# First norm by plain transposes, attention in pairs of banks, and values from high and low parts of the probabilities side by side

## The reference, cut to what matters

```
mod = silu(c) @ w_mod[l] + b_mod[l]
shift, scale, gate = split(mod, 3)
h = rms_norm(x, g_pre[l]) * (1.0 + scale) + shift
... = split(h @ w_in_e)                       # 2560 columns: GLA, latent attention, gates

s = einsum('qhd,khd->hqk', qn, kn) + einsum('qhr,kr->hqk', qr, kr)    # 4 heads, 2048 x 2048
p = softmax(s)
o = einsum('hqk,khd->qhd', p, v) * silu(z)
```

## Time and profile before

| | us |
|---|---|
| median of 3 runs | 3141.64 |
| lowest and highest run | 3140.18, 3143.88 |
| the profiled execution, its own time | 3143.72 |
| its span, first to last instruction | 3141.9 |
| PE busy | 3020.9 (96%) |
| DVE busy | 1365.7 (43%) |
| ACT busy | 1171.1 (37%) |
| POOL busy | 655.5 (21%) |

### The profile page before, as it was taken

How to read it: one execution, slowest core, us unless ns; L and a number is a source line. 1 busy time by engine, 2 the same in 40 slices (tenths; PEclk the granted TensorE clock), 3 DMA queues, 4 the chain that set the end, 5 groups by cost and what they waited for, 6 DMA issues and landing times.

```text
span 3141.9 us, 47947 instructions
## 1 busy us (share of the span) xinstructions
PE 3020.9 (96%) x17252; PEld 2534.5 (81%) x17252; DVE 1365.7 (43%) x2431; ACT 1171.1 (37%) x2092; POOL 655.5 (21%) x614
## 2 busy tenths in 40 slices
PE   4899999999899999998999999999999999999999
PEld 4668888888788888887878888888888888877887
DVE  5276777755676776673434111122222222222011
ACT  3462244555455555553235111232332332322111
POOL 2111211256222222221320001011211211113221
PEclk8999999999999999999999999999999999999999
DMA  6233345596221111122643211121121121134231
GB/s 228 71 118 97 109 153 160 161 285 197 74 58 54 53 54 53 54 58 91 207 167 118 94 74 50 61 81 60 60 80 60 60 80 60 53 134 160 95 107 53
DMA packets 259929, 317.65 MB, mean 101 GB/s; under 512 B 17187, under 2 KB 187299, under 8 KB 257220
## 3 DMA queue, kind: packets, MB, share of 16 engines
q1 hardware_dynamic: 259814, 316.10, 30.9%
HBM read 213.67 MB, written 102.37 MB: 101 GB/s over the span
## 4 chain that ended last, share of the span: by engine, by line
PE 87%; issue 4%; POOL 3%; DVE 3%; ACT 2%; DMA 1%; SPq 0%; POOLq 0%; DVEq 0%; ACTq 0%
PE PS L349 12%; PE PS L351 11%; PE PS L350 11%; PE PS L2287 4%; PE PS L2288 4%; PE PS L2289 4%; PE PS L2438 4%; PE PS L2439 4%; PE PS L2440 4%; PE PS L1739 4%; PE PS L1759 2%; PE PS L1760 2%; PE PS L1761 2%; PE PS L1728 2%; PE PS L1729 2%
## 5 line engine op out<-in xcount | busy, mean ns | idle before, releaser
L349 PE MATMUL PS<-hTh,whi 128*128 128x512 f32 x1664 | 661.1, 397 | 26.1 <-DVE hTl L302 15.7
L351 PE MATMUL PS<-hTh,wlo 128*128 128x512 f32 x1664 | 652.1, 392 | 0.0
L350 PE MATMUL PS<-hTl,whi 128*128 128x512 f32 x1664 | 652.0, 392 | 0.0
L349 PEld LDWEIGHTS PS<-hTh,whi 128*128 128x128 f32 x1664 | 315.1, 189 | 99.8 <-issue 15.2
L351 PEld LDWEIGHTS PS<-hTh,wlo 128*128 128x128 f32 x1664 | 315.0, 189 | 66.7
L350 PEld LDWEIGHTS PS<-hTl,whi 128*128 128x128 f32 x1664 | 315.5, 190 | 63.7 <-issue 0.2
L341 POOL TENSOR_TENSOR whi<-wraw,zero 128x1024 fp32r<-128x1024 f32 x52 | 100.2, 1928 | 1205.8 <-PE PS L351 953.3
L1832 ACT ACTIVATE pb__168<-PS,nm,rq 128x512 f32<-128x512 f32 x256 | 197.5, 780 | 130.1 <-DVE nm L1896 130.1
L2287 PE MATMUL PS<-ow_h,of_h 128*128 128x512 f32 x576 | 225.0, 391 | 7.5 <-DVE oy L2242 7.5
L2288 PE MATMUL PS<-ow_l,of_h 128*128 128x512 f32 x576 | 224.8, 390 | 0.0
L2289 PE MATMUL PS<-ow_h,of_l 128*128 128x512 f32 x576 | 224.7, 390 | 0.0
(11 more groups left out here) (268 smaller groups left out, 5850.5 us busy)
## 6 DMA issues: line engine op xcount, KB each, us to landing
projT<-pev SPq DMA_DIRECT2D x80, 256.0 KB, 2.7
xt<-x SPq DMA_DIRECT2D x8, 2048.0 KB, 9.4
mw<-wmod SPq DMA_DIRECT2D x64, 256.0 KB, 2.8
oxt<-x SPq DMA_DIRECT2D x32, 512.0 KB, 4.8
sg_v<-vev SPq DMA_DIRECT2D x64, 256.0 KB, 2.4
wraw<-wuz SPq DMA_DIRECT2D x32, 512.0 KB, 6.0
vm<-sg_v SPq DMA_DIRECT2D x16, 1024.0 KB, 5.6
sgT<-mT SPq DMA_DIRECT2D x16, 1024.0 KB, 4.4
```

The costliest lines, as they stand in the source:

```text
L349: pe.matmul(PS[:, bank, :], w[1][:, s, k, :], hTh[:, k, b], start=(k == 0), stop=False)
L350: pe.matmul(PS[:, bank, :], w[1][:, s, k, :], hTl[:, k, b], start=False, stop=False)
L351: mm = pe.matmul(PS[:, bank, :], w[2][:, s, k, :], hTh[:, k, b], start=False, stop=(k == KD - 1))
```

## The change

It has three parts.

**Start.** `norm_pool_scale` and `ndiag` are gone. DVE scales x in place (`norm_dve_scale`, which layer 1 already used) and PE does plain transposes. A block of the first eight waits for each feature step by itself. PE does all eight steps of a group's transposes together, after the second block of a pair. ACT squares the next group between steps 3 and 4 of a group. The first two weight tiles are loaded before the last four rows of w_mod; ACT makes their high part and DVE the low one. The rows for the gates are loaded later, and the modulation's buffers lie in a free part of hTh.

**Order of the attention.** PE: S0 S1 T0 T1 S2 S3 T2 T3 V0 V1, then S0 S1 T0 T1 S2 S3 shares V2 V3 T2 T3. ACT and DVE follow.

**Values and shares.** High and low parts lie side by side in `pt`, so a key step is a 512-wide matmul (v high by both parts) and a 256-wide one (v low by the high part). High-by-high and high-by-low land in two halves of bank 6; DVE multiplies each half by the gate and adds them (three instructions in place of one), and the next values wait for the two multiplications (`s_oa`). `diag` is split by POOL in `dgh` and `dgl`, and the shares are two 256-wide float32r matmuls.

```diff
-        macc0 = at("macc0", X0, [P, 2 * D])
-        mw0 = at("mw0", X0 + 8 * K, [P, 4, D])
+        macc0 = at("macc0", H0 + 36 * K, [P, 2, 2 * D])
+        mw0 = at("mw0", H0 + 4 * K, [P, 4, 2 * D])
...
-        def norm_pool_scale(pool, g):
-            pool.wait_ge(s_rs, 2 * g + 2)
-            if g:
-                pool.wait_ge(s_tp, 8 * g)
-            for t in range(4):
-                r = 40 + 4 * (g % 2) + t
-                pool.tensor_tensor(ndiag[:, t, :], ident[:, :], small[:, r:r + 1].broadcast_to([P, P]), ALU.mult).then_inc(s_xn, 1)
...
-                if g < 4:
-                    mm = pe.matmul(o, x, ndiag[:, t, :], start=True, stop=True)
-                else:
-                    mm = pe.transpose(o, x, ident[:, :])
+                mm = pe.transpose(o, x, ident[:, :])
...
             for k in range(KD):
+                if normed is not None:
+                    pe.wait_ge(s_hl, normed + k + 1)
...
+        def first_split_act(act, g):
+            act.wait_ge(s_wr[g], 16)
+            act.activation(whi0[:, g, :, :].rearrange("p k c -> p (k c)"), wraw0[:, g, :], ACT.Copy).then_inc(s_whi, 1)
+
+        def first_split_dve(dve, g):
+            dve.wait_ge(s_whi, g + 1)
+            dve.tensor_tensor(wlo0[:, g, :, :].rearrange("p k c -> p (k c)"), wraw0[:, g, :],
+                              whi0[:, g, :, :].rearrange("p k c -> p (k c)").bitcast(F32), ALU.subtract).then_inc(s_wlo, 1)
...
             for m in range(8):
                 norm_act(act, m)
+            norm_act_front(act, 1)
             for g in range(1, 4):
-                norm_act_front(act, g)
                 proj_evict(act, 2 * g - 2)
-                for k in range(6):
+                proj_evict(act, 2 * g - 1)
+                for k in range(8):
                     norm_act(act, 8 * g + k)
-                proj_evict(act, 2 * g - 1)
-                for k in range(6, 8):
-                    norm_act(act, 8 * g + k)
+                    if k == 3 and g < 3:
+                        norm_act_front(act, g + 1)
...
             for n in range(2 * KD):
                 mod_sum(dve, n)
+                if n == 4:
+                    norm_dve_scale(dve, 0)
+                if n == MOD_CUT:
+                    first_split_dve(dve, 0)
+                if n == MOD_CUT + 1:
+                    first_split_dve(dve, 1)
             mod_end(dve, 0)
             norm_dve(dve, 0)
             for g in range(1, 4):
+                norm_dve_scale(dve, g)
                 norm_dve(dve, g)
...
             for j in range(8):
                 proj_block(pe, j)
-                g = j // 2 + 1
-                if g < 4:
-                    for k in (range(6, 8) if j % 2 else range(6)):
-                        norm_pe(pe, 8 * g + k)
+                if j % 2 and j < 7:
+                    for k in range(8):
+                        norm_pe(pe, 4 * j + 4 + k)
...
-                for u in range(2):
-                    mm = pe.matmul(PS[:, 7, u * P:(u + 1) * P], ones[:, :], diag[:, u, :], start=True, stop=True)
-                mm.then_inc(s_rb, 1)
+                both = ones[:, :].bitcast(F32R)
+                pe.matmul(PS[:, 7, 0:2 * P], both, dgh[:, :, :].rearrange("p u c -> p (u c)"), start=True, stop=False)
+                pe.matmul(PS[:, 7, 0:2 * P], both, dgl[:, :, :].rearrange("p u c -> p (u c)"), start=False, stop=True
+                          ).then_inc(s_rb, 1)
...
-                    o, tok = PS[:, 6, 0:2 * P], slice(k * P, (k + 1) * P)
-                    pe.matmul(o, vh[:, tok], pth[:, k, :], start=(k == 0), stop=False)
-                    pe.matmul(o, vh[:, tok], ptl[:, k, :], start=False, stop=False)
-                    mm = pe.matmul(o, vl[:, tok], pth[:, k, :], start=False, stop=(k == NT - 1))
+                    tok = slice(k * P, (k + 1) * P)
+                    pe.matmul(PS[:, 6, :], vh[:, tok], pt[:, k, :, :].rearrange("p a q -> p (a q)"), start=(k == 0), stop=False)
+                    mm = pe.matmul(PS[:, 6, 0:2 * P], vl[:, tok], pt[:, k, 0, :], start=False, stop=(k == NT - 1))
...
-                dve.tensor_tensor(ost[:, :], PS[:, 6, 0:2 * P], mzt[:, :], ALU.mult).then_inc(s_oe, 1)
+                dve.tensor_tensor(ost[:, :], PS[:, 6, 0:2 * P], mzt[:, :], ALU.mult).then_inc(s_oa, 1)
+                dve.tensor_tensor(mzt[:, :], PS[:, 6, 2 * P:4 * P], mzt[:, :], ALU.mult).then_inc(s_oa, 1)
+                dve.wait_ge(s_oa, I * 2 + (E_oa + 5))
+                dve.tensor_tensor(ost[:, :], ost[:, :], mzt[:, :], ALU.add).then_inc(s_oe, 1)
...
                 pool.tensor_tensor(diag[:, u, :], ident[:, :], rinv[:, u:u + 1].broadcast_to([P, P]), ALU.mult).then_inc(s_dg, 1)
+                pool.wait_ge(s_dg, N * 3 + 7)
+                pool.tensor_tensor(dgh[:, u, :], diag[:, u, :], zero[:, 0:1].broadcast_to([P, P]), ALU.add).then_inc(s_dg, 1)
+                pool.wait_ge(s_dg, N * 3 + 8)
+                pool.tensor_tensor(dgl[:, u, :], diag[:, u, :], dgh[:, u, :].bitcast(F32), ALU.subtract).then_inc(s_dg, 1)
```

More of the change, by code:

```diff
@@ L172, in mod_sum @@
                 dve.wait_ge(s_macc, n)
-            acc = macc0[:, half * D:(half + 1) * D]
-            dve.scalar_tensor_tensor(acc, mw0[:, n % 4, :], cvec[:, k:k + 1], acc, ALU.mult, ALU.add).then_inc(s_macc, 1)
+            acc = macc0[:, half, 0:D]
+            dve.scalar_tensor_tensor(acc, mw0[:, n % 4, 0:D], cvec[:, k:k + 1], acc, ALU.mult, ALU.add).then_inc(s_macc, 1)
         def mod_cols(pe, acc, half):
-            for j in range(half * KD, half * KD + KD):
-                mm = pe.matmul(PS[:, 0, j:j + 1], acc[:, j * P:(j + 1) * P], ones[:, 0:1], start=True, stop=True)
+            for k in range(KD):
+                j = half * KD + k
+                mm = pe.matmul(PS[:, 0, j:j + 1], acc[:, k * P:(k + 1) * P], ones[:, 0:1], start=True, stop=True)
             return mm
@@ L184, in mod_pe @@
                 pe.wait_ge(s_macc, KD * (half + 1))
-                mm = mod_cols(pe, macc0, half)
+                mm = mod_cols(pe, macc0[:, half, 0:D], half)
             mm.then_inc(s_mps, 1)
@@ L391, in start_sp @@
             norm_load(sp, 0, (0,))
-            for n in range(2 * KD):
+            for n in range(MOD_CUT):
+                mod_load(sp, n)
+            for g in range(2):
+                proj_load(sp, g)
+            for n in range(MOD_CUT, 2 * KD):
                 mod_load(sp, n)
@@ L395, in start_sp @@
             sp.wait_ge(s_macc, 2 * KD)
-            for g in range(2):
-                proj_load(sp, g)
+            gate_rows(sp)
             norm_load(sp, 0, (2,))
@@ L406, in start_act @@
             norm_act_front(act, 0)
+            for g in range(2):
+                first_split_act(act, g)
             for m in range(8):
                 norm_act(act, m)
+            norm_act_front(act, 1)
             for g in range(1, 4):
-                norm_act_front(act, g)
                 proj_evict(act, 2 * g - 2)
-                for k in range(6):
+                proj_evict(act, 2 * g - 1)
+                for k in range(8):
                     norm_act(act, 8 * g + k)
-                proj_evict(act, 2 * g - 1)
-                for k in range(6, 8):
-                    norm_act(act, 8 * g + k)
+                    if k == 3 and g < 3:
+                        norm_act_front(act, g + 1)
             proj_evict(act, 6)
@@ L432, in start_pool @@
             pool.wait_ge(s_const, 48)
-            norm_pool_front(pool, 0)
-            norm_pool_scale(pool, 0)
-            pool.wait_ge(s_mps, 1)
-            for g in range(2):
-                proj_split(pool, g)
-            for g in range(1, 4):
+            for g in range(4):
                 norm_pool_front(pool, g)
-                norm_pool_scale(pool, g)
         def start_pe(pe):
@@ L1609, in emit @@
         pb_ = at("pb_", M0 + 111 * K, [P, 2, S])
-        pth = at("pth", M0 + 127 * K, [P, NT, 2 * P], F32R)
-        ptl = at("ptl", M0 + 143 * K, [P, NT, 2 * P], F32R)
+        pt = at("pt", M0 + 127 * K, [P, NT, 2, 2 * P], F32R)
+        dgh = at("dgh", M0 + 64 * K, [P, 2, P], F32R)
+        dgl = at("dgl", M0 + 65 * K, [P, 2, P], F32R)
         qraw = at("qraw", M0 + 68 * K, [P, 2, 2, P])
@@ L1666, in emit @@
         s_oe = sem("s_oe")
+        s_oa, E_oa = s_bk, NT
         s_mlg = sem("s_mlg")
@@ L1708, in mod1_pe @@
             for half in range(2):
-                mod_cols(pe, macc1, half)
+                mod_cols(pe, macc1[:, half * D:(half + 1) * D], half)
             for bank, src in ((1, macc1[:, 2 * D:2 * D + 512]), (2, macc1[:, 2 * D + 512:]), (3, maccg[:, 0:512]), (4, maccg[:, 512:])):
@@ L1783, in pieces @@
                                 piece_pe(pe, n)
-                    for b in range(2):
-                        scores(h, N, u, (b,))
-                        turn_if(b)
+                    scores(h, N, u, (0, 1))
+                    turn_if(0)
+                    turn_if(1)
                     if u:
```

65 lines of the change are left out of this document (31 added, 34 removed).

## The result

| | before | after |
|---|---|---|
| median, runs (us) | 3140.93, 4 runs | 3112.91, 4 runs |
| lowest to highest | 3140.18 to 3143.88 | 3108.08 to 3116.9 |
| the profiled execution | 3143.72 | 3112.22 |
| its span | 3141.9 | 3110.4 |

What follows compares the result with a forecast made beforehand. TensorE holds 87% of the chain, so its list sets the time nearly everywhere. Attention 13.8 us plus start 12.3 make 26.1 us saved, giving 3115.5 us by the median, range 3104 to 3131.

Steps and rivals of the forecast that it cites:

- Values, 0.13 us a pair: Attention values on PE: a 512-wide and a 256-wide matmul per key step save 16 issues, 0.13 us a pair.
- Rival 4: Attention: wide value steps held by weight loads, narrow shares costing as float32; 3127 to 3130 us, chance 0.11 with rival 2.
- Shares, 0.20: Attention shares on PE: two 256-wide float32r matmuls take 0.24 us, saving 0.20 us a pair.
- Waits for the low part, 0.10: Attention turns on PE: the paired order leaves nothing of the 0.10 us a pair spent waiting for VectorE's low part.
- Changing between turns and scores costs PE nothing: Attention on PE: 1.16 us of scores plus 0.44 of transposes make the 1.60 measured, so pairing saves no switching price.
- GpSimd, 0.3 us of room: Attention: with two more GpSimd instructions, the query split still ends 0.3 us before PE's next first scores, at no cost.
- VectorE's room: Attention: despite two more instructions, VectorE's low parts are read some 0.3 to 0.7 us before the turns need them.
- rival 2: Attention: VectorE late, third and fourth turns wait 0.4 us a pair, no attention gain; 3129 us, chance 0.11 with Rival 4.
- Until the modulation, +1.2 us: Start: VectorE's added scalings and subtractions end the modulation 1.2 us after 43.94 us, bounds 0 and 2.6.
- First group: Start: low-part contention between VectorE and POOL goes; transposes of the second group start at 63.5 us, against 66.45.
- Groups 2 to 4, 59.8 and 3 us for the clock: Start: groups take 21.5, 21.5 and 16.8 us, plus 1 us each for half clock; eighth block ends at 126.3.
- rival 1: Start: half clock through all three second blocks loses 14.7 us, so the start gives 0.6; 3127 us, chance 0.13.

Runs made afterwards that it cites:

- the added operation: The changed kernel with one more GpSimd operation of 128 columns behind each low part of the inverse sums, result unused: 3122.75 us.
- the variant of three moves: Changed kernel with low parts behind VectorE's last modulation sum, second group's squares before the first norm, six next-group transposes between a group's two blocks: 3106.88 us.
- the one of two moves: The variant of three moves with the low parts of the first weight tiles put back between VectorE's modulation sums: 3104.62 us.
- the kernel with the whole wait: The changed kernel, but the first block of a group waits for all eight norm steps, as before, not step by step: 3136.82 us.
- the store moved: The variant of three moves with the first block's result stored before the last 2 MB of x are loaded, not behind them: 3103.88 us.

## Why the prediction was right, and where its steps were off

The forecast was 3115.5 us in a range of 3104 to 3131; 3112.9 was measured, faster, by the mechanisms it named. That the two are so near is in part luck. Between the two profiled executions the gain is 31.5 us and the sum had 26.1: the pairs gave 3.0 us more than forecast, the start 0.6, and the stages outside both 1.7, for which the sum had nothing. Step by step:

- **Values, 0.13 us a pair.** 0.13 by the two periods 18.68 and 18.55. Held. Rival 4 did not come: a key step takes 0.35 us and the shares 0.24.
- **Shares, 0.20.** 0.20 by 18.88 and 18.68. Held.
- **Waits for the low part, 0.10.** 0.10, at the one turn named above. Held.
- **"Changing between turns and scores costs PE nothing"** was the sentence that failed, and it made pairing them worth nothing in the sum. I had read it from one turn and one run of five scores, and could not see there that in runs of ten the later steps are shorter. That gave another 0.10 us a pair: it came out at 18.55 and not 18.65, 3 us of the kernel.
- **What the sum hid.** The three terms were added as if each stood alone. They don't: the values and the shares are worth nothing without the order. The total was near because all three were made together; the prediction has no sentence that says so.
- **GpSimd, 0.3 us of room.** 0.11 by the added operation. The chain from the shares to the end of the split came within 0.1 us of what I had worked out (3.63 us from 1117.54 to 1121.17, where I had 3.55), and I had left out the handing over (0.12 us from the split's end to the scores where PE waits). Right in kind, close to wrong in effect: a quarter of a microsecond more on GpSimd would have cost 4 to 5 us (0.14 by 32).
- **VectorE's room.** From 860 to 1390 us no wait of PE for the low part is left; rival 2 did not come.
- **Until the modulation, +1.2 us.** It was +3.1, beyond my bound of 2.6: I had priced VectorE's two subtractions (which stand three and two sums from the end, not four), and not that w_mod's rows arrive behind the weight tiles. In the variant of three moves, with the subtractions behind the last sum, it was still 45.5: 1.6 us for the rows, and 1.5 for the subtractions.
- **First group.** ACT's start to group 2's transposes was 17.4 us (47.26 to 64.66) where I had 18.2. With the later modulation the transposes came at 64.66 instead of 63.5.
- **Groups 2 to 4, 59.8 and 3 us for the clock.** 60.9 in all: 22.8, 21.6 and 16.5. The half clock struck in the first blocks' pauses (0.77 over 75 to 90 us) and not through the second blocks, which took 5.8, 5.5 and 5.4 us: rival 1 did not come. The eighth block ended at 125.6, forecast 126.3: two misses of 1.2 and 1.9 us with opposite signs.
- **What the start's sum did not weigh.** I let PE follow step by step and set no price on it. It is worth 24.3 us, and the old place of the transposes, with the squares moved, is worth 7.3 more on top of it.
- **The range.** The forecast's own upper end, 3121, doesn't follow from its bound of 3 us for the start, which gives 3125.

The Trainium skill, TensorE: Matmul & The Clock Gate, Back-to-back issue gap, gives 2.5 ns beyond the columns; it calls this the gap of an isolated matmul, which in a stream with weight loads counts too little for few columns and too much for many. A step of the wide values is 0.348 us (mean of six, from 1109.63 to 1111.72) for 768 columns, which are 0.320 at 2.4 GHz, so 14 ns for each of the two: here the trace doesn't agree, it is above the 2.5 for both together. By that figure the values would have given 0.04 us a pair; they gave 0.13.

## What to carry to other kernels

An edit that shortens an engine's list pays only where no other engine's pace is the next limit; before dropping an edit that measured nothing alone, see in the waits whether its time came back as a wait, and try it together with the edit that frees that wait. When a wait is made finer, ask what the old arrangement did with the same pause: here the old interleaving together with the new wait step by step (and the squares moved) ended the eighth block at 118 us, the new wait without it at 126. And look at what a small store stands behind in its DMA queue when something waits for the store.

## What the runs showed of the hardware

The same two query tiles, with the same instructions, took 4.3 us less in one variant than in another by their clock alone. They are the first and the third at the attention's opening, in the variant of three moves:

```profile
783.20:799.80 16.60, 14.22 (x45) 9.91 (x46) 7.57 (x13) 6.88 (x15) 4.83 (x3) 0.83 0.43 126
816.20:827.00 10.80, 10.80 (x53) 9.15 (x54) 6.00 (x11) 4.20 (x9) 3.06 (x6) 0.84 0.14 38
```

and in the one of two moves, where the clock stayed at 1.0 (2.4 GHz) through both:

```profile
784.80:798.70 13.90, 11.51 (x44) 7.96 (x45) 7.51 (x13) 6.89 (x15) 4.84 (x3) 1.00 0.41 116
815.10:824.30 9.20, 9.20 (x53) 7.96 (x54) 6.07 (x11) 4.13 (x9) 3.10 (x6) 1.00 0.15 45
```

PE's waits at the opening are the same in both (8.5 us in all), and in the kernel with the whole wait the two tiles took 13.9 and 9.2 us too. So between kernels that differ only at the start, some 4 us at one place can come from where the clock falls. Other places can take some of it back: of these 4.3 us 2.6 are left at the first shares (829.8 and 832.4), since the way from the eighth block to the opening took 1.5 us more. This is why 3104.6 and 3106.9 don't rank those two variants. With the store moved the two tiles took 13.9 and 12.0 us, 1.5 less, and the way to the opening 1.5 more.

A GpSimd multiplication by the diagonal took 0.40 us behind the shares and 0.87 beside VectorE's sum; the Trainium skill, SBUF — State Buffer, Who interferes with whom, has this as a lock between the two, and the trace agrees in kind. The two new operations fell outside it: all 64 of each took 0.40 and 0.46 us.
